# Head squares and sums inside the head projection, and a gate tile in place of constant matmuls

## The reference

```python
# second block, attention mixer, in short
h = rmsnorm(x) @ w_in              # queries (16 heads), keys (2), values (2), gate (1024)
q = rmsnorm_per_head(q) * q_norm
k = rmsnorm_per_head(k) * k_norm
p = softmax(q @ k.T - slope * distance, with a sink per head)
out = (p @ v * silu(gate)) @ w_out
```

## Time and profile before

| | us |
|---|---|
| median of 3 runs | 1663.57 (1662.13 to 1666.88) |
| the profiled execution | 1663.52 |
| its span, first to last instruction | 1661.8 |
| TensorE busy in the span | 1603.5 |
| VectorE busy | 1169.3 |
| ScalarE busy | 907.4 |
| head projection, first tile's start to last tile's end | 1106.01 to 1139.50 |
| heads stage, up to the first scores | 1139.50 to 1158.09 |
| attention units, up to the output product | 1158.09 to 1229.40 |

### The profile page before, as it was taken

How to read it: one execution, slowest core, us unless ns; L and a number is a source line. 1 busy time by engine, 2 the same in 40 slices (tenths; PEclk the granted TensorE clock), 3 DMA queues, 4 the chain that set the end, 5 groups by cost and what they waited for, 6 DMA issues and landing times. The chain is left out here.

```text
span 1661.8 us, 33818 instructions
## 1 busy us (share of the span) xinstructions
PE 1603.5 (96%) x12970; PEld 1435.4 (86%) x12970; DVE 1169.3 (70%) x2011; ACT 907.4 (55%) x1622; POOL 74.1 (4%) x41
## 2 busy tenths in 40 slices
PE   7999899999999999999999999998999999999998
PEld 6888788999999999998888888887667889988877
DVE  5678566689888999986666666655765657656565
ACT  4357554454555767766566656653664645334443
POOL 0000000200000000000000000000001333200000
PEclk9999999999999999999999999999999999999999
DMA  6642255565654444446666666643122444300014
GB/s 224 190 134 86 89 165 152 168 187 160 188 183 150 142 129 139 130 139 206 197 191 192 193 195 190 192 134 98 57 75 75 152 152 152 118 25 3 3 32 147
DMA packets 63222, 230.02 MB, mean 138 GB/s; under 512 B 7024, under 2 KB 7280, under 8 KB 63104
## 3 DMA queue, kind: packets, MB, share of 16 engines
q1 hardware_dynamic: 63104, 228.37, 44.3%
HBM read 227.30 MB, written 1.05 MB: 137 GB/s over the span
## 5 line engine op out<-in xcount | busy, mean ns | idle before, releaser
L1140 DVE TENSOR_TENSOR tile_low<-weights,tile_high 128x1024 fp32r<-128x1024 f32 x252 | 308.0, 1222 | 141.3 <-ACT tile_high L1130 141.2
L1130 ACT ACTIVATE tile_high<-weights 128x1024 fp32r<-128x1024 f32 x252 | 268.0, 1064 | 134.0 <-issue 134.0
L183 ACT ACTIVATE tile_high<-weights 128x1024 fp32r<-128x1024 f32 x169 | 178.5, 1058 | 239.5 <-issue 62.9
L195 DVE TENSOR_TENSOR tile_low<-weights,tile_high 128x1024 fp32r<-128x1024 f32 x146 | 179.9, 1233 | 138.7 <-ACT tile_high L183 121.9
L1212 PE MATMUL banks<-parts,tile_high 128*128 128x256 f32 x2048 | 272.0, 286 | 0.9 <-ACT tile_high L1130 0.6
L1212 PEld LDWEIGHTS banks<-parts,tile_high 128*128 128x128 f32 x2048 | 255.3, 192 | 1.7 <-issue 1.7
L1532 PE MATMUL banks<-tile_high,parts 128*128 128x512 f32 x1024 | 253.0, 389 | 0.9 <-ACT parts L1490 0.9
L1532 PEld LDWEIGHTS banks<-tile_high,parts 128*128 128x128 f32 x1024 | 192.2, 188 | 40.9 <-issue 1.1
L237 PE MATMUL banks<-parts,tile_high 128*128 128x272 f32 (+1 forms) x1216 | 168.5, 291 | 2.3 <-ACT big L317 2.3
L237 PEld LDWEIGHTS banks<-parts,tile_high 128*128 128x128 f32 x1216 | 157.2, 190 | 11.3 <-issue 7.5
L1217 PE MATMUL banks<-parts,tile_low 128*128 128x256 f32 x1024 | 144.3, 284 | 4.1 <-DVE tile_low L1140 4.0
(11 more groups left out here) (402 smaller groups left out, 2177.7 us busy)
## 6 DMA issues: line engine op xcount, KB each, us to landing
weights<-in_peer_u SPq DMA_DIRECT2D x128, 512.0 KB, 3.6
weights<-in_peer_v SPq DMA_DIRECT2D x128, 512.0 KB, 3.5
weights<-in_dn_in SPq DMA_DIRECT2D x49, 512.0 KB, 3.5
weights<-in_in_t SPq DMA_DIRECT2D x19, 512.0 KB, 3.5
weights<-in_attn_t SPq DMA_DIRECT2D x19, 512.0 KB, 3.6
weights<-in_in_m SPq DMA_DIRECT2D x16, 512.0 KB, 3.7
weights<-in_wq SPq DMA_DIRECT2D x16, 512.0 KB, 3.7
weights<-in_dn_out SPq DMA_DIRECT2D x16, 512.0 KB, 3.5
```

The source lines that it names most:

```text
L183: k.nc.scalar.activation(k.high[:, m % 2, :], k.ring.view(n), ACT.Copy).then_inc(*k.high_made.up())
L195: unit.tensor_tensor(k.low[:, m % 2, :], k.ring.view(n), k.high[:, m % 2, :].bitcast(F32), ALU.subtract).then_inc(*k.low_made[engine].up())
L1130: k.nc.scalar.activation(k.high[:, (s + j) % 2, :], k.ring.buf[:, j % RING, :], ACT.Copy).then_inc(k.high_made.sem, 1)
L1140: k.nc.vector.tensor_tensor(k.low[:, (s + j) % 2, :], k.ring.buf[:, j % RING, :], k.high[:, (s + j) % 2, :].bitcast(F32), ALU.subtract).th ...
```

## The change

The squares and sums of the head normalisation move into the projection's loop: behind tile i, TensorE sums head tile i-1, and ScalarE squares it ahead of its next `make_high`. Tiles use seven banks, since bank 7 holds the sums. Projection and heads stage become one block without a barrier between; TensorE waits for the copy of V instead. In the heads stage the six constant matmuls go, and the first gate tile is computed in full in their place; ScalarE copies it out behind the root and then makes the high half of the third gate tile, ahead of the spread's end. In the attention the remaining seven gate tiles fill units 0 to 7 and 10 to 15. The halves made there move: high and low of gate tiles 3 to 7 and of the first output tile in units 2, 4, 6, 8, 12 and 14, and the low half of gate tile 2 in unit 1.

```diff
@@ project_T, tensor
             for i in range(chunks):
-                if i >= 8:
-                    pe.wait_ge(*by[engine(i - 8)].at(nth[i - 8]))
+                if i >= banks:
+                    pe.wait_ge(*by[engine(i - banks)].at(nth[i - banks]))
...
+                if beside is not None and i:
+                    beside["tensor"](pe, i - 1)
@@ project_T, scalar
             for i in range(chunks):
+                if beside is not None and i:
+                    act.wait_ge(*by["vector"].at(i))
+                    beside["scalar"](act, i - 1)
                 if i + AHEAD < chunks:
                     make_high(act, k, first + i + AHEAD)
@@ sink_attention_stage
+    filled = [*range(8), *range(10, 16)]
     gate_tile = lambda i: k.tiles["attn_g"] + i
-    ahead = dict(zip(range(2, 16, 2), [gate_tile(i) for i in range(AHEAD, fills)] + [k.tiles["attn_out"]]))
+    ahead = dict(zip((2, 4, 6, 8, 12, 14), [gate_tile(i) for i in range(3, fills)] + [k.tiles["attn_out"]]))
@@ tensor
-                if u < 2 * fills:
-                    if u and u % 2 == 0:
-                        pe.wait_ge(*gated.at(u // 2))
-                    tile_piece(pe, k, gate_tile(u // 2), fill, lambda c: (high[:, c, :], low[:, c, :]), u % 2, 2)
+                if u in filled:
+                    f = filled.index(u)
+                    if f and f % 2 == 0:
+                        pe.wait_ge(*gated.at(1 + f // 2))
+                    tile_piece(pe, k, gate_tile(1 + f // 2), fill, lambda c: (high[:, c, :], low[:, c, :]), f % 2, 2)
@@ vector
+                if u == 1:
+                    make_low(dve, k, gate_tile(2))
                 if u in ahead:
                     make_low(dve, k, ahead[u])
@@ scalar
-                if u and u % 2 == 0:
-                    act.wait_ge(k.ring.used.sem, gate_tile(u // 2 - 1) + 1)
-                    nc.scalar.activation(T[:, GATE + u // 2 - 1, :], fill, ACT.Copy).then_inc(*gated.up())
+                if u - 1 in filled and filled.index(u - 1) % 2:
+                    q = 1 + filled.index(u - 1) // 2
+                    act.wait_ge(k.ring.used.sem, gate_tile(q) + 1)
+                    nc.scalar.activation(T[:, GATE + q, :], fill, ACT.Copy).then_inc(*gated.up())
@@ heads_stage, scalar
-            for c in range(n):
-                if c >= 2:
-                    act.wait_ge(*summed.at(c - 1))
-                nc.scalar.activation(sq[:, c % 2, :], xs[c], ACT.Square).then_inc(*squared.up())
-                if c == 4:
-                    make_high(act, k, second)
+            make_high(act, k, second)
             act.wait_ge(*vec.at(1))
             nc.scalar.activation(r[:, 1, :], r[:, 0, :], ACT.Sqrt).then_inc(*rooted.up())
+            act.wait_ge(k.ring.used.sem, first_gate + 1)
+            nc.scalar.activation(k.T2[:, 10, :], ps[:, 6, 0:L], ACT.Copy).then_inc(*gated.up())
             nc.scalar.activation(k.norms[:, 47:48], k.norms[:, 47:48], ACT.Exp).then_inc(*exped.up())
+            make_high(act, k, first_gate + 2)
@@ heads_stage, tensor
+            pe.wait_ge(*evacuated.last())
             for i, (c0, rows) in enumerate(spans):
                 nc.tensor.transpose(ps[0:rows, i, 0:P], k.vT2[:, c0:c0 + rows], k.ident).then_inc(*turned.up())
-            pe.wait_ge(*k.fetched.last())
-            for c in range(n):
-                pe.wait_ge(*squared.at(c + 1))
-                nc.tensor.matmul(ps[0:SUMS, 7, 0:L], k.c("pair")[:, 18 - 2 * c:18 - 2 * c + SUMS], sq[:, c % 2, :], start=c == 0,
-                                 stop=c == n - 1).then_inc(*summed.up())
-            keep_busy(k, 6, 6)
+            tile_T(pe, k, first_gate, ps[:, 6, 0:L], lambda c: (high_x[:, c, :], low_x[:, c, :]))
...
+                if c == 6:
+                    pe.wait_ge(*gated.at(1))
@@ second_block
+    def square_head(act, c):
+        if c >= 2:
+            act.wait_ge(*summed.at(c - 1))
+        nc.scalar.activation(sq[:, c % 2, :], xs[c], ACT.Square).then_inc(*squared.up())
+
+    def sum_head(pe, c):
+        if c == 0:
+            pe.wait_ge(*k.fetched.last())
+        pe.wait_ge(*squared.at(c + 1))
+        nc.tensor.matmul(ps[0:SUMS, 7, 0:L], k.c("pair")[:, 18 - 2 * c:18 - 2 * c + SUMS], sq[:, c % 2, :], start=c == 0,
+                         stop=c == len(xs) - 1).then_inc(*summed.up())
 
     with k.joined():
-        meta = heads_stage(k, [k.T2[:, c, :] for c in range(10)], lambda c: k.p("q_norm") if c < 8 else k.p("k_norm"), spans)
+        project_T(k, "attn_t", N_ATTN, L,
...
+                  k.tiles["attn_g"] + RING, norm, following="attn_g", banks=7,
+                  beside={"tensor": sum_head, "scalar": square_head})
+        meta = heads_stage(k, xs, lambda c: k.p("q_norm") if c < 8 else k.p("k_norm"), spans, squared, summed)
```

More of the change, by code:

```diff
@@ L414, in norm_programs, with project_T @@
             "turned": turned}
-def project_T(k, name, chunks, n, write, prefetch, norm, following=None):
+def project_T(k, name, chunks, n, write, prefetch, norm, following=None, banks=8, beside=None):
     nc, ps, first = k.nc, k.ps, k.tiles[name]
@@ L436, in _ @@
             for i in range(chunks):
-                if i >= 8:
-                    pe.wait_ge(*by[engine(i - 8)].at(nth[i - 8]))
+                if i >= banks:
+                    pe.wait_ge(*by[engine(i - banks)].at(nth[i - banks]))
                 if n == S:
-                    tile_both(pe, k, first + i, ps[:, i % 8, :], n, norm if i == 0 else None)
+                    tile_both(pe, k, first + i, ps[:, i % banks, :], n, norm if i == 0 else None)
                 else:
-                    tile_T(pe, k, first + i, ps[:, i % 8, 0:n], lambda c: (high[:, c, :], low[:, c, :]),
+                    tile_T(pe, k, first + i, ps[:, i % banks, 0:n], lambda c: (high[:, c, :], low[:, c, :]),
                            norm=norm if i == 0 else None)
+                if beside is not None and i:
+                    beside["tensor"](pe, i - 1)
         @block.vector
@@ L452, in _ @@
                     dve.wait_ge(k.ring.used.sem, first + i + 1)
-                    put(dve, i, ps[:, i % 8, 0:2 * n if n == S else n]).then_inc(*by["vector"].up())
+                    put(dve, i, ps[:, i % banks, 0:2 * n if n == S else n]).then_inc(*by["vector"].up())
                 if following is not None and i == chunks - 2:
@@ L464, in _ @@
                     act.wait_ge(k.ring.used.sem, first + i + 1)
-                    put(act, i, ps[:, i % 8, 0:n]).then_inc(*by["scalar"].up())
+                    put(act, i, ps[:, i % banks, 0:n]).then_inc(*by["scalar"].up())
             if following is not None:
@@ L1624, in sink_attention_stage @@
     scaled, turned, unturned, summed = k.start("att_scaled", "att_turned", "att_copied", "att_valued")
-    stored, stats, gated = k.start("att_stored", "att_stats", "gate_made")
+    stored, stats = k.start("att_stored", "att_stats")
+    gated = k.signals["gate_made"]
     fills = AH // 2
+    filled = [*range(8), *range(10, 16)]
     gate_tile = lambda i: k.tiles["attn_g"] + i
-    ahead = dict(zip(range(2, 16, 2), [gate_tile(i) for i in range(AHEAD, fills)] + [k.tiles["attn_out"]]))
+    ahead = dict(zip((2, 4, 6, 8, 12, 14), [gate_tile(i) for i in range(3, fills)] + [k.tiles["attn_out"]]))
     high, low = k.pair(L)
@@ L1815, in sink_attention_stage, with heads_stage @@
     return last_values
-def heads_stage(k, xs, weights, spans):
+def heads_stage(k, xs, weights, spans, squared, summed):
     nc, ps, T = k.nc, k.ps, k.T2
     n, AK, m = len(xs), 8, META
-    squared, summed, vec, rooted, wide, applied = k.start("head_squared", "head_summed", "head_vector",
-                                                          "head_rooted", "head_spread", "head_applied")
+    vec, rooted, wide, applied, gated = k.start("head_vector", "head_rooted", "head_spread", "head_applied", "gate_made")
+    evacuated = k.signals["evacuated_vector"]
+    first_gate, high_x, low_x = k.tiles["attn_g"], *k.pair(L)
     turned, copied, picked = k.start("values_turned", "values_copied", "picks_made")
     product, meta, exped = k.start("meta_product", "meta_vector", "meta_exped")
-    sq, r = k.squares2, k.factors[0:SUMS]
+    r = k.factors[0:SUMS]
     pick = lambda c: k.picks[0:SUMS, P * c:P * c + P]
@@ L1974, in second_block @@
     V = 10
-    project_T(k, "attn_t", N_ATTN, L,
-              (lambda i: "vector", lambda eng, i, src: nc.vector.tensor_copy(k.vT2 if i == V else k.T2[:, i, :], src)),
-              k.tiles["attn_g"] + RING, norm, following="attn_g")
     spans = [(0, META)] + [(META + tt * P, P) for tt in range(NT)]
-    if stop <= 22: return
-    with k.joined():
-        meta = heads_stage(k, [k.T2[:, c, :] for c in range(10)], lambda c: k.p("q_norm") if c < 8 else k.p("k_norm"), spans)
+    xs, sq = [k.T2[:, c, :] for c in range(10)], k.squares2
+    squared, summed = k.start("head_squared", "head_summed")
+    def square_head(act, c):
[8 more added lines that the diff above has]
```

(7 more changed lines are left out.)

## The result

Over twenty runs each, the changed kernel takes 1668.31 us in the median and the kernel before 1664.43; the ratio is 1.0023 (95% interval 1.0014 to 1.0032). That is slower by 3.9 us, outside the range on record. The prediction had taken about 0.3% as the least that a measurement tells from no change; with twenty runs each, the interval leaves out 1 at 0.23%. The profiled execution took 1666.78 us.

A forecast was written before the change was run, and what follows sets the result against it. The prediction took TensorE to bound the projection and VectorE to lead in the attention. Gains of 1.1 (heads) and 1.05 (attention) less 1.5 (clock) made 0.65 us off, forecasting 1662.9 us; range 1660.0 to 1666.5, chance 0.90.

The forecast's parts named there:

- the term for the clock: Attention units 8 to 10: one fall to half clock of about 3.4 us, costing 1.5 us.
- rival (2): Spread and attention both lose clock cover: falls cost 1.7 and 3.4 us, total 1666.5 us; chance 0.20.
- the rule of the Trainium skill: TensorE before the spread: idling halves the clock, so the 3.25 us gap would bring a fall, giving rival (2)'s time.
- the prediction's own signs of being wrong: Projection tiles over 3.65 us apart, attention shorter by over 2 us, or clock falls both before the spread and in attention.
- The gain in the heads stage: Projection to spread: sums at 0.48 us each, a low half newly on the path; spread starts 1.1 us sooner.
- Unit 1: Attention unit 1: VectorE's added low half delays turn(2) by 1.23 us, and nothing later absorbs it.
- Unit 10: Attention unit 10: VectorE loses a low half and its wait; unit 12's low half starts 2.3 us sooner, kept to the end.
- rival (3): Attention bound by TensorE, so the gate tile's 3.3 us are gained whole, with 1.1 before: 1659.1 us; chance 0.08.

The follow-up runs named there:

- e1: Changed kernel with four constant matmuls added in TensorE's gap between the first gate tile and the spread; ratio to the kernel before 1.0002.
- e3: Changed kernel with four constant matmuls before the spread and two each in attention units 8 and 9; ratio to the kernel before 0.9991.
- e7: Kernel before with the first gate tile replacing the six constants and the attention's new filling; squares and sums not moved; ratio 1.0007.
- e6: Kernel before with only squares and sums moved into the projection, blocks joined; six constants and old attention kept; ratio 1.0010.
- e9: e6 with nine constant matmuls before the spread instead of six; median 1661.13 us, ratio to the kernel before 0.9982.
- e10: e6 with the low half of the second gate tile made by GpSimd and eight constants instead of six; ratio to the kernel before 0.9985.
- e8: e3 with the low half of gate tile 2 made by GpSimd in the heads stage instead of VectorE in unit 1; ratio to the kernel before 1.0002.
- e4: The changed kernel itself timed again, nothing altered, against the kernel before; median 1665.98 us, ratio 1.0014.
- e2: Changed kernel with two constant matmuls each in attention units 8 and 9, none before the spread; ratio to the kernel before 1.0009.

## Why the prediction was wrong

**The step that failed is the term for the clock.** The sum took one fall of 3.4 us at a price of 1.5. The profile has three, 13.6 us in all. Their places: the spread (price 1.68 us, 6.51 less 4.83; rival (2) had 1.7), unit 2 (0.4 us: turn(2) at +15.08, in e1 at +14.68), and units 9 to 10 (1.6 us of turn(12) against e3). Together 3.7 us, the stage's 125.24 less e3's 121.54, where the sum had 1.5. Rival (2) was the right mechanism; it missed only unit 2, and it had 0.20. Its weight was mis-set by an argument in it: that the dense gate tile just ahead would hold the clock through the gap. A gap of 1.75 us behind that tile (e7) and one of 2.37 us behind constants (e6) were followed by a fall, gaps of 0.44 (e9), 0.65 (e1) and 0.87 us (before) were not. For the rule of the Trainium skill quoted in the prediction (TensorE: Matmul & The Clock Gate, Why this matters for your kernels) the trace agrees: a gap of 3.23 us, then 0.50 from 1155.5 on. Of the prediction's own signs of being wrong, the last came true: the clock fell at both places.

**The gain in the heads stage** was right in kind and forecast too small: 1.1 us, measured 1.64. The sum was priced at 0.48 and measured 0.45, and the low half delays the step by 1.13 us, not 1.23. It is on the path as said (e10).

**The attention.** Unit 1: +1.12 us for +1.23, kept up to turn(8) (e8 takes it back). Unit 10: 2.3 us forecast; with TensorE at full clock e3 shows 0.8 between turn(8) and turn(12), and its rows leave room for at most 1.7 without constants. What the bare order is worth at full clock was never seen, since without filler the clock fell there in all four profiles (changed, e4, e1, e7). That TensorE would be late next behind VectorE was right, but the term was mis-sized: it let the low half of unit 12 wait for gate tile 5 alone. In e3 it waits for its high half, and that stands in ScalarE's program behind the copies of turn(10)'s rows and the exponentials, and so behind TensorE, whose turn(10) starts at 1206.37:

```profile
1207.22 0.37 ACT L1800 ACTIVATE big<-banks 16x256 f32<-16x256 f32 x1 [0.47 <-PE banks L1689]
...
1209.23 1.04 ACT L183 ACTIVATE tile_high<-weights 128x1024 fp32r<-128x1024 f32 x1
...
1210.31 1.23 DVE L195 TENSOR_TENSOR tile_low<-weights,tile_high 128x1024 fp32r<-128x1024 f32 x1 [2.99 <-ACT tile_high L183]
```

The low half starts 52.24 us behind the first scores, where it started 51.94 us behind them before: 0.8 us are gained on the 1.1 of unit 1, and not 2.3. Against the attention of before without a fall (70.87 us in e9), that of e3 is 0.27 us longer and not 1.05 shorter; of this, up to 0.9 us are its constants.

**From the profile to the median.** The sum was made against one execution of the kernel before whose clock had stood at 1.00 through the stage. The falls make a kernel's time a spread and not a number: before, the runs of the first comparison reach from 1661.8 to 1667.1, and among the 35 beside e1 to e4 the 16 with a mean clock of 0.991 have a median of 1662.8 us, the 5 at 0.988 one of 1669.2. The changed kernel's runs never had more than 0.989; at 0.989 their median is 1664.4 us, at 0.983 1671.2. The profile's stage is 1.85 us longer than before and the medians differ by 3.9, while the second comparison (e4) has 1.7. Longer falls, such as e4's (stage 128.3 us), may explain the rest; that is argued and not measured. Time outside the stage moves as well: ahead of it both kernels run the same 7186 matmuls, yet the projection starts at 1106.0 us before and at 1109.5 after, and between 1106.0 and 1112.5 in the fourteen profiles; behind it 432.4 and 429.7 us pass.

**The terms side by side.** Up to the scores the stage gained 1.68 us at full clock (e3), where 1.1 were forecast. The attention lost 0.27 with constants, where a gain of 1.05 was forecast. The falls cost 3.7 us, where 1.5 were forecast, and the kernel before paid 0.44 for its own at the stage's end. That makes +1.85 us, as the profile has it, against -0.65. So with all falls away the change frees 1.4 us and not 2.15, and the clock takes more than that back. Between the last two terms up to 0.9 us may shift, since e3's constants stand in both.

**The range and the chances.** The prediction says that no case reaches a bound by its own sum. But rival (2) comes to 1666.5, which is the upper bound, and rival (3) to 1659.1, below the lower one. With 0.08 outside for (3) and about half of the 0.20 of (2), some 0.8 would have been the chance of the range, and not 0.90.

## What to carry to other kernels

Before useless matmuls are taken out, or useful ones moved away, look at what TensorE does on both sides of the hole: price the hole at the half clock of what follows it, place by place. A longer wait by itself is no such hole yet: TensorE's 1.86 us in unit 1 were followed by a fall only in profiles in which the spread had fallen before. Moving work onto an engine that is full pays only if the stretch it leaves is filled again; e9 has the first part's gain for three more constant matmuls. And where falls come and go between executions, compare many runs, and take a stage's length from profiles with the clock beside it.

## What was not expected of the hardware

- A plain fp32 matmul of two records set between tiles of the cheaper kind costs 0.45 us, no more than in a dense row of its own (0.48): no price for the change of kind shows.
- GpSimd makes a low half in 2.35 us where VectorE needs 1.23, and VectorE is not slowed beside it: in e10 the copies of V and the first step on the sums, which lie within GpSimd's time, take 0.67 and 0.42 us as in the changed kernel without it, and in e8 the ten steps of the application, which begin while GpSimd works, take 4.56 us in all as before.
- With constants of 2.6 us in a hole of two units the clock stayed at 1.00 there in one profile (e3) and not in two (e2, e8). A cover that works in one execution is not yet a cover.
